# TensorE's expert loop written out, in a two-block transformer kernel on one core

## What is computed

```
def _swiglu(x, w1, w3, w2):
    return (jax.nn.silu(x @ w1) * (x @ w3)) @ w2

def _moe(x, w_router, w1, w3, w2):
    logits = (xt @ w_router).astype(jnp.float32)
    top_v, top_e = lax.top_k(logits, TOP_K)
    gates = jax.nn.softmax(top_v, axis=-1)
    ...
    yb = lax.map(run, ...)          # _swiglu of an expert's tokens with w1[e], w3[e], w2[e]
    y = zeros.at[stok].add(yb[dest] * sg)
```

## Time and profile before

| | before |
|---|---|
| median of 3 runs | 2975.96 us |
| the profiled execution, its own time | 2980.48 us |
| its span, first to last instruction | 2978.7 us |
| mean granted TensorE clock | 0.974 of full speed |
| expert stage, first up to last down on TensorE | about 2008 to 2930 us |
| instruction records | 70710 |

### The profile page before, as it was taken

One profiled execution on the slowest core, in us unless ns is written; L12 is line 12 of the kernel. 1 busy time (PEld: TensorE's weight loads), 2 busy tenths in 40 slices (PEclk: granted clock), 3 DMA queues, 4 the chain that ended last, 5 costly groups with the idle time before them and its releaser, 6 DMA issues.

```text
span 2978.7 us, 70710 instructions
## 1 busy us (share of the span) xinstructions
PE 2820.9 (95%) x32594; PEld 2322.8 (78%) x32594; DVE 714.0 (24%) x1336; ACT 355.0 (12%) x778; POOL 9.4 (0%) x21
## 2 busy tenths in 40 slices
PE   7998999999999999979998999789999999999997
PEld 6776788887677667846775678559999999999995
DVE  0001454533677333420002234220000000000002
ACT  1001231210100023200000223010000000000000
POOL 0000000000000000000000000000000000000000
PEclk9999999899999999989998999899999999999999
DMA  4434232013243433323434233319999999999993
GB/s 184 169 127 171 100 138 100 4 48 137 111 169 145 152 116 113 125 105 127 169 128 167 103 138 112 122 43 375 381 394 380 375 386 361 384 391 373 372 395 120
DMA packets 54130, 596.58 MB, mean 200 GB/s; under 512 B 6097, under 2 KB 6353, under 8 KB 8289
## 3 DMA queue, kind: packets, MB, share of 16 engines
q1 hardware_dynamic: 52272, 588.43, 50.5%
q0 software_dynamic: 1712, 5.93, 0.6%
HBM read 593.29 MB, written 1.05 MB: 200 GB/s over the span
## 4 chain that ended last, share of the span: by engine, by line
PE 92%; DVE 4%; DMA 2%; issue 1%; ACT 1%; SPq 0%; DVEq 0%; ACTq 0%
PE bank L307 20%; PE bank L2130 19%; PE bank L398 15%; PE bank L2142 9%; PE bank L315 7%; PE bank L409 7%; PE bank L1054 2%; DMA slot<-in_experts 2%; PE bank L1336 1%; PE bank L2223 1%; PE bank L1348 1%; PE bank L374 1%; PE bank L2175 1%; PE bank L1710 1%; PE bank L1037 0%
## 5 line engine op out<-in xcount | busy, mean ns | idle before, releaser
L2130 PE MATMUL bank<-arena,slot 128*64 128x96 f32 x14336 | 618.0, 246 | 8.9 <-issue 7.5
L2130 PEld LDWEIGHTS bank<-arena,slot 128*64 128x64 f32 x14336 | 603.7, 137 | 12.7 <-issue 12.1
L398 PE MATMUL bank<-h_cm,slot 128*128 128x256 f32 x2112 | 464.2, 381 | 4.1 <-DVE h_cm L350 2.8
L307 PE MATMUL bank<-h_cm,slot 128*128 128x256 f32 (+1 forms) x2064 | 457.2, 383 | 3.6 <-DVE h_cm L352 2.3
L398 PEld LDWEIGHTS bank<-h_cm,slot 128*128 128x128 f32 x2112 | 403.3, 191 | 72.5 <-issue 18.6
L307 PEld LDWEIGHTS bank<-h_cm,slot 128*128 128x128 f32 (+1 forms) x2064 | 393.4, 191 | 67.4 <-issue 12.5
L2142 PE MATMUL bank<-ff,slot 128*64 128x96 f32 x7168 | 324.2, 247 | 12.4 <-DMA slot<-in_experts 7.3
L2142 PEld LDWEIGHTS bank<-ff,slot 128*64 128x64 f32 x7168 | 310.6, 138 | 14.8 <-issue 14.8
L2290 DVE TENSOR_TENSOR ff<-ff,bank 128x192 f32<-128x192 f32 x112 | 39.7, 354 | 802.4 <-PE bank L2130 802.4
L409 PE MATMUL bank<-slot,ff 128*128 128x512 f32 x528 | 231.5, 592 | 0.0
L409 PEld LDWEIGHTS bank<-slot,ff 128*128 128x128 f32 x528 | 100.3, 190 | 113.5 <-issue 111.9
(11 more groups left out here) (352 smaller groups left out, 1697.5 us busy)
## 6 DMA issues: line engine op xcount, KB each, us to landing
slot<-in_experts SPq DMA_DIRECT2D x112, 2048.0 KB, 8.7
slot<-in_experts SPq DMA_DIRECT2D x112, 1024.0 KB, 8.8
slot<-in_ffn SPq DMA_DIRECT2D x22, 2048.0 KB, 9.2
slot<-in_ffn SPq DMA_DIRECT2D x22, 1024.0 KB, 4.9
slot<-in_dense SPq DMA_DIRECT2D x11, 2048.0 KB, 8.9
slot<-in_dqk SPq DMA_DIRECT2D x8, 2048.0 KB, 8.6
slot<-in_g SPq DMA_DIRECT2D x8, 2048.0 KB, 8.0
slot<-in_w_in_rkv SPq DMA_DIRECT2D x6, 2048.0 KB, 7.9
```

Source lines behind the costliest of these rows:

```text
L307: ins = pe.matmul(ps[0:m, j * S:(j + 1) * S], w[:, k * width + c0:k * width + c0 + m], rhs[:, k, :], start=k == 0, stop=k == ks - 1)
L398: ins = pe.matmul(bank[:, m * S:(m + 1) * S], slot[s][:, c0:c0 + P], h_cm[:, k, :], start=k == 0, stop=k == KD - 1)
L2130: ins = pe.matmul(bank[64 * c:64 * c + 64, m * PLACES:(m + 1) * PLACES], slot[s][:, c0:c0 + 64], QUEUE[:, e, k, :], start=k == 0, stop=k = ...
```

## The change

One line. The loop of six rounds on TensorE is no longer a loop on the engine; Python writes its body six times, with `i` as a number. The code of the seven other stages, the other engines' loops and all DMAs of weights stay as they are.

```diff
                     down(0, 0, start=True)
                     if e:
                         pe_moe_turn(pe, p, e - 1)
-                    with pe.Fori(0, U_EXPERT // 2 - 1) as i:
+                    for i in range(U_EXPERT // 2 - 1):
                         up(i, 2)
                         down(i, 1)
                         up(i, 3)
```

## The result

| | before | after |
|---|---|---|
| median | 2973.82 us (4 runs) | 3023.64 us (4 runs) |
| ratio of after to before, 95% interval | | 1.0176 (1.0151 to 1.0201) |
| the profiled execution, its own time | 2980.48 us | 3022.41 us |
| its span | 2978.7 us | 3020.6 us |
| expert stage: first up to first matmul of line 2223 | 2008.25 to 2934.89: 926.6 us | 1999.99 to 2976.77: 976.8 us |

The kernel is 50 us slower, and in the profiled executions the expert stage alone is 976.8 - 926.6 = 50.1 us longer. The spans differ by 41.9 us only because the older execution reached the stage 8.3 us later. The page's clock row has an 8 in the slice from 521 to 596 us in the one and a 9 in the other, far ahead of the stage, so I compare the stage and not the span.

The account below looks back on a forecast made before the run. TensorE sets the pace, with DMA engines full beside it. 120 borders at 0.79 us (95 us) less 7.3 us gave +87.5 on 2980.5, 3068 us, less 4.5 to the median: 3063 us; 3029 to 3112 at 50%, range 3010 to 3140.

Parts of the forecast that it names:

- air for half: Expert stage: DMA engines get ahead, only every second packet border meets weights, at half the middle price; +40 us, 3016 us, 19%.
- Packets: Expert stage: five more copies of the round per expert add 30720 instructions, 120 packets of 256.
- Removed jumps back: TensorE's loop of rounds: five jumps back per expert go; they showed no gap, so 0 us.
- Weight waits gone: End of each expert, before downs: waits for weight loads vanish because loads get ahead; -7.3 us.
- Price per border: TensorE at each new 256-instruction border in the expert stage: 0.79 us stall, 120 of them, 95 us.
- the upper bound: Times between two stalling borders in the old stage: 6.70, 6.07, 6.90, 7.67 us; mean 6.84, 1.57 us over 5.27.
- A sign that I gave: Changed expert stage: forecast wrong if packets come without gaps, or gaps are not one packet (127 or 128 MATMULs) apart.
- the other signs: Expert stage: 160 to 165 packets, 60 to 150 us issue idle, DMA share 0.8 to 0.9, weight waits near zero.
- Feedback: Expert stage: a stall slows TensorE but not the weights, so some fetches are fast; pulls border cost down from 1.57 us.
- Faster: Expert stage: gaps belong to loop entry and exit, straight code arrives early; 12.6 and 7.3 us go, 2956 us, 8%.
- only bytes: Expert stage: fetches hide, 2 MB of new code stretch the saturated DMA engines; +5 us, 2981 us, 6%.

Follow-up runs that it names:

- light twins: Changed kernel and the kernel before, each expert weight load cut to its first quarter of columns: 2946.05 us and 2943.49 us.
- wide kernel: Changed kernel with 128 places per expert in place of 96: 3239.89 us; the kernel before with the same edit: 3237.17 us.

## Why the prediction was right, and where it was off

The direction, the place and the mechanism of a late fetch held. 3063 us was forecast and 3023.64 measured: +50 us where +87.5 was summed. That is inside 3010 to 3140, but below the 3029 to 3112 us that carried half of the chance. The range held it only because its low end took in the rival "air for half", to which I gave 19%.

- *Packets*: 120 expected, 121 counted. Right.
- *Removed jumps back at 0 us*: right by the light twins, 897.9 and 898.7 us.
- *Weight waits gone*: -7.3 expected, -5.7 measured. Right in kind.
- *Price per border*: this is the term that was mis-sized. 0.79 us was taken; the shown issue gaps give 42.6 / 121 = 0.35 us, the whole stage with the weights' 5.7 us added back (50.1 + 5.7) / 121 = 0.46 us. The single late fetches were sized well: gaps after are 0.2 to 1.8 us, 0.85 us in the mean of 65, and the wide kernel shows that 7.0 us between borders are enough. What I took wrong is how often. I laid the 12.6 us on the last two borders ahead of the rounds, 16 in all, and they don't all belong there. Counted in MATMULs, at least four of the 13 gaps, 4.5 us (at 2493.06, 2599.61, 2607.28 and 2714.44), lie at earlier borders; the others are 8.1 us, 0.50 for each of the 16. Laid on all code of the old stage, some 49 packets, the 12.6 us are 0.26 us per border. In the changed stage 65 of some 165 borders have a gap, since in steady rounds most borders fall at good points of the load cycle. Of the four pairs behind the upper bound, the one of 7.67 us has the transposes between its borders; its stall was 1.35 us and not 2.40. The rival "air for half" said one in two at half the price, +40 us. It came nearer than the forecast, by luck in part: two in five are late, and at the full price.
- *A sign that I gave, and the record*: the forecast was to be wrong if the gaps were not one packet apart. As a rule they aren't: 19 of 64 distances are one packet, 30 are three. The sign was too strict, since a border in time between two late ones breaks it and not the mechanism; that each gap ends with a packet is what had to be seen. Of the other signs the packets (170 in the stage for 160 to 165, before 50 for 48) and the weight waits (1.6 us) came out nearly as said, the gaps (55.2 us for 60 to 150) and the DMA share (0.93 for 0.8 to 0.9) just outside.
- *Feedback* (a stall gives the fetches air): consistent with the share's fall from 0.99 to 0.93, but the runs don't separate it from the fixed pattern of three. With three quarters of the weights there are still 28 gaps, which says that air alone doesn't do it.
- *"Faster"* (gaps belong to entry and exit of the loop) is out by the light twins, and *"only bytes"* by the same: the 2 MB more are there at no cost.
- The Trainium skill calls the cost of a block border "mostly hidden" ("Runtime: NRT & Kernel Launch", section Instruction fetch mechanics). That is right for these runs with light loads or wide matmuls and wrong at 5.27 us per border under full weight traffic. The same section of the Trainium skill says that a taken branch to a block that isn't held stalls until it is fetched. The gaps of 5.27 to 6.81 us with three rounds bear it out, and the kernel with one expert per turn shows that a target that is held costs nothing. In "Advanced Engine Details and Errata", section ISA Cache, the Trainium skill gives two cache lines. TensorE shows more: 1536 instructions stay, 2304 don't.

## What to carry to other kernels

Before writing out an engine loop, compare the time in which the engine works off 256 instructions with the time of a code fetch under the kernel's own traffic. Here it was 5.27 us against 5.4 to 7.1 for the late ones, and the loop that was held in store cost nothing. Look at the instruction rows of the DMA queues: a stretch without packets is code that is held. Gaps that the profile puts down to "issue" and that lie whole multiples of 256 instructions apart are late packets. Where straight code in a busy stretch shows such gaps, let a loop turn over more of the work, so that less code is fetched, up to what the store holds and not beyond. Here one expert per turn fetched 37 packets less and gained 0.4%. A larger body alone isn't that: two written rounds fetched 24 packets more and lost 0.5%, three didn't fit and lost 4.1%.

## What the hardware showed that I had not expected

- A loop slightly too large for the store is the worst of all forms: 3092 us against 2974 (held) and 3024 (written out). Part of it is the clock: in the 5.3 to 6.8 us that TensorE stands still at each jump back, the granted clock falls to 0.50 and stays there for some 4 us of the work that follows.
- TensorE goes on 2.2 to 2.5 us after the start of the packet that it waited for, at all 65 gaps.
- Halving the weight packets made the code fetch later (63.8 us of gaps against 55.2) and left the loop kernel as it was.
- The late fetches follow the load cycle: 43 of the 49 borders crossed 0.4 to 3 us after a 2 MB issue had a gap at the next border, against 6 of the 59 crossed later than 3 us after an issue.
- The profile's idle time of the matmuls shows only three quarters of such a loss (38 of 50 us); the weight loads' idle time shows 47.7.
